# A float32 transformer pair on one core: how the products of `w_down_2` are split and ordered at the end

## The chip, the cores and the metric

One Trainium2 chip, one of its cores. The time is the device time of one execution in microseconds (us); the kernel before took 1609.27 us in the median of three runs (1608.09 to 1610.73).

## The reference, cut to what matters

Two transformer blocks on one sequence of 512 tokens with a model width of 1024. The change touches only the end of the second block, its MLP:

```python
h2 = rmsnorm(x, mlp_norm_w[l])
u = jax.nn.relu(jnp.einsum('bld,df->blf', h2, w_up[l]))
x = x + jnp.einsum('blf,fd->bld', u * u, w_down[l])
return rmsnorm(x, final_norm_w)
```

Here `w_up_2` is 1024 x 4096 and `w_down_2` is 4096 x 1024, both float32.

## The kernel before

The program writes an instruction stream for each engine by hand, with semaphores between them. Every float32 product is made of three TensorE products in a reduced float format: each operand is split into a high part (`hi`, a rounded copy, made by ScalarE, here called ACT) and a low part (`lo` = operand - `hi`, a subtraction), and `three` (L812 to L814) multiplies hi by hi, hi by lo and lo by hi into the same PSUM bank.

The end of the kernel is a list of 42 steps, `STREAM` (L246), that all engines walk through. There are two kinds of step.

- An **up unit** `("up", q, j)` is 256 columns of `w_up_2`: 48 matmuls for two PSUM banks. VectorE (DVE) takes each bank with a relu into `f` (L2230), and ACT squares it (L1688). Four units make the 1024 hidden columns of set q. The first two units of set 0 lie before the list.
- A **product** `("down", q, n)` is one of the seven products of a Strassen-Winograd scheme that multiplies the 512 x 1024 hidden values of set q by 1024 rows of `w_down_2`: 24 matmuls for two banks. `PRODUCTS` names its operands: token parts A11 to A22 and sums S1 to S4 (128 x 1024 each), weight parts B11 to B22 and sums T1 to T4 (128 x 2048). Products of one chain (`CHAIN`) accumulate in the same two banks, and DVE adds the running sum of a bank to `x` after each product (L2237), so the next product of the chain may start in a bank only once DVE has taken it (`claim_tail`, L1241).

Before a step v can start on PE, its weights need: a load from HBM into one of five 1 MB places (`raw`, `raw_tail`; `load_tail`, issued by SP in the order of the list, each waiting until the low part of the step that held the place is made, and after n = 3 or 4 also until T4 or T3 is made, L717); for a sum, the subtraction on DVE (`weight_sum`, L2249 to L2261); the high part on ACT (`tail_high`, L1664); and the low part. The low part is made on GpSimd (POOL) in two halves of 128 x 1024 (L795, L797), except for n = 2, where DVE makes it in one instruction (`weight_low`, L2297). A product also needs the token part: high on ACT (`token_high`, L1680), low on DVE (`token_low`, L2290), and for S1 to S4 a sum on DVE (`token_sum`, L2271 to L2282).

The order on each engine is written out per step `at_v`: ACT squares the second half of the step before, makes the weights' high part of step `at_v + 2`, then its tokens' high part, then squares the first half of `at_v`. DVE takes the second half of the step before, makes sums, makes the low parts of step `at_v + 2`, and only then takes the first half of `at_v` (loop at L2300). High and low parts have three places each in rotation, so step v + 2 can be prepared once step v has started. The order of the steps is: units of set 0 and 1; the seven products of set 0; four units of set 2; seven products of set 1; four units of set 3; seven products of set 2; seven products of set 3:

```python
for q in range(2, FF2_Q):
    out += down[q - 2] + up[q]
return out + down[FF2_Q - 2] + down[FF2_Q - 1]
```

## Time and profile before

| what | before |
|---|---|
| median of three runs | 1609.27 us |
| the profiled execution, its own time | 1609.46 us |
| its span | 1607.6 us |
| PE busy | 1563.9 us, 97% of the span |
| DVE, ACT, POOL busy | 916.2, 531.6, 790.2 us |
| mean granted TensorE clock | 0.99 |
| the list of 42 steps on PE | 1250 to 1600 us |

The span is what the profiler saw between first and last instruction; the execution's own time is 1.9 us more. In the view of instructions in order of time, the first matmul of set 0 starts at 1315.68 us, the units behind it at 1364.69, set 1 at 1408.21, the units behind it at 1455.87, set 2 at 1499.39, set 3 at 1551.38, and the last matmul's slot ends at 1600.37.

### The profile page before, as it was taken

The numbers are of one execution on the slowest core, as the hardware profiler recorded it, in microseconds if no ns is written. First come the engines' busy times: TensorE is split into PE (matmuls) and PEld (weight loads), VectorE is DVE, ScalarE is ACT, GpSimd is POOL, SyncE is SP. The second block draws the span as 40 slices with busy tenths as digits, with TensorE's granted clock in tenths as the row PEclk, the third lists the DMA queues.
The fourth block names the chain that finished last, engine by engine and source line by source line (L and its number), as shares of the span: only waits on it lengthen the run. The fifth ranks groups of instructions, "written<-read, shape, count | busy, mean of one in ns | idle before, by whom it ended". The sixth has DMA issues, their size and how long they took to land.

```text
span 1607.6 us, 19248 instructions
## 1 busy us (share of the span) xinstructions
PE 1563.9 (97%) x7495; PEld 1286.0 (80%) x7495; DVE 916.2 (57%) x1185; ACT 531.6 (33%) x760; POOL 790.2 (49%) x289
## 2 busy tenths in 40 slices
PE   9999999999999999999999999999999998989886
PEld 7887788888888888888888887877789886868764
DVE  5902588900246666666006489987555156382798
ACT  3012121200135443443124244257433334242334
POOL 5874288677760445445440003421251448556476
PEclk9999999999999999999999999999999999999998
DMA  6232032233242332332232232221232503214021
GB/s 223 90 120 79 1 112 92 92 105 105 79 131 80 105 105 79 104 104 89 95 118 73 89 97 79 81 52 26 80 131 79 183 27 127 83 56 154 0 79 53
DMA packets 127382, 147.00 MB, mean 91 GB/s; under 512 B 5143, under 2 KB 98375, under 8 KB 127304
## 3 DMA queue, kind: packets, MB, share of 16 engines
q1 hardware_dynamic: 125430, 141.05, 27.9%
q10 hardware_dynamic: 1874, 4.85, 0.9%
q8 instruction: 55, 0.90, 0.3%
q14 instruction: 23, 0.19, 0.0%
HBM read 143.79 MB, written 2.10 MB: 91 GB/s over the span
## 4 chain that ended last, share of the span: by engine, by line
PE 85%; POOL 5%; DVE 4%; issue 3%; ACT 2%; DMA 1%; POOLq 0%; DVEq 0%; SPq 0%; ACTq 0%
PE ps L812 26%; PE ps L814 25%; PE ps L813 25%; PE ps L967 3%; PE ps L1042 2%; POOL w_lo L795 1%; POOL w_lo L797 1%; PE ps L1209 1%; POOL w_lo L759 1%; PE ps L1030 1%; POOL tail_lo L795 1%; PE ps L1226 1%; DVE a_lo L2290 1%; POOL w_hi L754 1%; DVE x L2237 1%
## 5 line engine op out<-in xcount | busy, mean ns | idle before, releaser
L759 POOL TENSOR_TENSOR w_lo<-raw,w_hi 128x1024 fp32r<-128x1024 f32 x166 | 420.5, 2554 | 496.4 <-ACT w_hi L1312 493.6
L812 PE MATMUL ps<-hT_hi,w_hi 128*128 128x512 f32 (+1 forms) x848 | 324.5, 383 | 0.8 <-POOL w_lo L759 0.5
L813 PE MATMUL ps<-hT_lo,w_hi 128*128 128x512 f32 (+1 forms) x848 | 323.2, 381 | 0.0
L814 PE MATMUL ps<-hT_hi,w_lo 128*128 128x512 f32 (+1 forms) x848 | 323.2, 381 | 0.0
L754 POOL TENSOR_TENSOR w_hi<-raw,cells 128x2048 fp32r<-128x2048 f32 x35 | 129.5, 3701 | 126.5 <-PE ps L812 125.3
L812 PEld LDWEIGHTS ps<-hT_hi,w_hi 128*128 128x128 f32 x848 | 159.4, 188 | 33.9 <-issue 2.3
L814 PEld LDWEIGHTS ps<-hT_hi,w_lo 128*128 128x128 f32 x848 | 159.4, 188 | 30.6
L813 PEld LDWEIGHTS ps<-hT_lo,w_hi 128*128 128x128 f32 x848 | 159.4, 188 | 30.4
L1312 ACT ACTIVATE w_hi<-raw 128x2048 fp32r<-128x2048 f32 (+1 forms) x58 | 109.6, 1890 | 128.3 <-PE ps L812 106.5
L812 PE MATMUL ps<-w_hi,hT_hi 128*128 128x512 f32 (+2 forms) x400 | 151.6, 379 | 0.0
L813 PE MATMUL ps<-w_lo,hT_hi 128*128 128x512 f32 (+2 forms) x400 | 150.1, 375 | 0.0
L814 PE MATMUL ps<-w_hi,hT_lo 128*128 128x512 f32 (+2 forms) x400 | 150.1, 375 | 0.0
L1787 DVE TENSOR_TENSOR w_lo<-raw,w_hi 128x1024 fp32r<-128x1024 f32 (+1 forms) x20 | 22.0, 1144 | 144.4 <-ACT w_hi L1312 144.4
L812 PEld LDWEIGHTS ps<-w_hi,hT_hi 128*128 128x128 f32 x400 | 75.4, 189 | 13.7 <-POOL w_lo L778 0.5
L814 PEld LDWEIGHTS ps<-w_hi,hT_lo 128*128 128x128 f32 x400 | 75.4, 188 | 13.3
L813 PEld LDWEIGHTS ps<-w_lo,hT_hi 128*128 128x128 f32 x400 | 75.4, 189 | 12.7
L812 PE MATMUL ps<-w_hi,a_hi 128*128 128x512 f32 x152 | 63.9, 421 | 18.8 <-POOL w_lo L797 18.8
L2290 DVE TENSOR_TENSOR a_lo<-f,a_hi 128x1024 fp32r<-128x1024 f32 x24 | 58.3, 2429 | 33.4 <-ACT a_hi L1680 33.4
L795 POOL TENSOR_TENSOR w_lo<-raw,w_hi 128x1024 fp32r<-128x1024 f32 x12 | 32.7, 2721 | 90.1 <-ACT w_hi L1664 90.1
L2230 DVE TENSOR_SCALAR f<-ps 128x512 f32<-128x512 f32 x28 | 19.0, 687 | 86.5 <-PE ps L814 86.5
L795 POOL TENSOR_TENSOR w_lo<-raw_tail,w_hi 128x1024 fp32r<-128x1024 f32 x14 | 44.7, 3194 | 40.0 <-ACT w_hi L1664 39.9
L813 PE MATMUL ps<-w_lo,a_hi 128*128 128x512 f32 x152 | 62.5, 411 | 0.0
(368 smaller groups left out, 3161.7 us busy)
## 6 DMA issues: line engine op xcount, KB each, us to landing
raw<-in_w_in SPq DMA_DIRECT2D x86, 512.0 KB, 4.7
raw<-in_w_up SPq DMA_DIRECT2D x60, 512.0 KB, 4.8
raw<-in_w_down SPq DMA_DIRECT2D x34, 512.0 KB, 4.2
raw_tail<-in_w_down SPq DMA_DIRECT2D x20, 512.0 KB, 4.7
raw<-in_w_out SPq DMA_DIRECT2D x16, 512.0 KB, 4.2
raw_tail<-in_w_up SPq DMA_DIRECT2D x16, 512.0 KB, 4.9
raw<-in_w_ret_o SPq DMA_DIRECT2D x8, 512.0 KB, 4.0
raw<-in_w_sgu_o SPq DMA_DIRECT2D x8, 512.0 KB, 4.0
```

The lines of the kernel that those rows point to most:

```text
L754: nc.gpsimd.tensor_tensor(hi[:, 0:n], raw[:, s, 0:n], zero.broadcast_to([P, n]), ALU.add).then_inc(unit_hi, 1)
L759: nc.gpsimd.tensor_tensor(lo[:, c], raw[:, s, c], hi[:, c].bitcast(f32), ALU.subtract).then_inc(unit_split, 1)
L795: nc.gpsimd.tensor_tensor(lo[:, 0:UNIT // 2], tail_raw_of(v)[:, 0:UNIT // 2], hi[:, 0:UNIT // 2].bitcast(f32), ALU.subtract)
L812: first = nc.tensor.matmul(dst, a_hi, b_hi, start=start, stop=False, skip_group_check=onto)
L813: nc.tensor.matmul(dst, a_hi, b_lo, start=False, stop=False, skip_group_check=onto)
L814: return first, nc.tensor.matmul(dst, a_lo, b_hi, start=False, stop=stop, skip_group_check=onto)
L967: last = nc.tensor.transpose(ps[:, BANK[t], n * width:n * width + width], src, ident[0:k, 0:k])
L1042: last = nc.tensor.matmul(ps[:, BANK[t], nn * 256:nn * 256 + 256], sT[:, h % 2, mb, n0:n0 + P], v[:, mb, h * RET_DV:(h + 1) * RET_DV], sta ...
L1312: nc.scalar.activation(slot_of(u)[0][:, 0:n], raw[:, s, 0:n], ACT.Copy).then_inc(hi_given, 1)
L1787: V.tensor_tensor(lo[:, c], raw[:, u % 2, c], hi[:, c].bitcast(f32), ALU.subtract).then_inc(unit_split, 1)
L2230: V.tensor_scalar(f2[q % 2][:, c, :], ps[:, TAIL_BANK[e], :], 0.0, None, ALU.max).then_inc(tail_taken, 1)
L2290: V.tensor_tensor(a_lo[:, a_n % A_SLOTS, :, :], tokens_of(q, PRODUCTS[n].split()[0]), a_hi[:, a_n % A_SLOTS, :, :].bitcast(f32), ALU.subtr ...
```

## The change

Four of the seven low parts of a set (n = 2, 3, 5, 6) are made on DVE in place of one; POOL keeps n = 0, 1 and 4, and all up units. The seven products of sets 1 and 2 no longer stand together: the units of the set after next stand between them (`BETWEEN`). Sets 0 and 3 are still seven products in a row. On ACT the tokens' high part now comes before the weights' high part of the same step. The sums T2 to T4 are tied to the step before their product; for products in a row that is the same place as before.

```diff
--- before.py
+++ after.py
@@ -230,27 +230,29 @@
 CHAIN = {0: "a", 1: "b", 2: "c", 3: "a", 4: "c", 5: "a", 6: "a"}
 OPENS = (0, 1, 2)
 TO_X = ((0, 0), (0, 0), (2, 1), (0, 1), (0, 1), (2, 1), (2, 0))
-VECTOR_LOW = 2
+VECTOR_LOW = (2, 3, 5, 6)
+BETWEEN = (("up", 0), ("down", 0), ("down", 1), ("up", 1), ("down", 2), ("down", 3), ("up", 2), ("down", 4), ("up", 3),
+           ("down", 5), ("down", 6))
 
 
 def second_mlp():
 
     up = [[("up", q, j) for j in range(4)] for q in range(FF2_Q)]
     down = [[("down", q, n) for n in range(7)] for q in range(FF2_Q)]
-    out = up[0][2:] + up[1]
-    for q in range(2, FF2_Q):
-        out += down[q - 2] + up[q]
-    return out + down[FF2_Q - 2] + down[FF2_Q - 1]
+    out = up[0][2:] + up[1] + down[0]
+    for q in range(1, FF2_Q - 1):
+        out += [up[q + 1][n] if kind == "up" else down[q][n] for kind, n in BETWEEN]
+    return out + down[FF2_Q - 1]
 
 
 STREAM = second_mlp()
-START = [STREAM.index(("down", q, 0)) for q in range(FF2_Q)]
+AT = {step: v for v, step in enumerate(STREAM)}
 RAW_SLOTS, W_SLOTS, A_SLOTS = 5, 3, 3
 
 
 def low_count(v):
 
-    by_vector = [kind == "down" and n == VECTOR_LOW for kind, _, n in STREAM]
+    by_vector = [kind == "down" and n in VECTOR_LOW for kind, _, n in STREAM]
     return by_vector[v], by_vector[:v + 1].count(by_vector[v])
 
 
@@ -1673,7 +1675,7 @@
                 else:
                     act.wait_ge(tokens_added, 4 * q + TOKEN_SUMS.index(name) + 1)
                 if a_n >= A_SLOTS:
-                    before = START[(a_n - A_SLOTS) // 7] + (a_n - A_SLOTS) % 7
+                    before = AT["down", (a_n - A_SLOTS) // 7, (a_n - A_SLOTS) % 7]
                     act.wait_ge(tail_started, before + 2)
                 else:
                     act.wait_ge(tail_started, 1)
@@ -1697,9 +1699,9 @@
                 if at_v:
                     square(at_v - 1, 1)
                 if at_v + 2 < N:
-                    tail_high(at_v + 2)
                     if STREAM[at_v + 2][0] == "down":
                         token_high(at_v + 2)
+                    tail_high(at_v + 2)
                 square(at_v, 0)
             root_table()
             for tt in range(2):
@@ -2245,18 +2247,18 @@
                 if name == "T1":
                     await_loaded(dve, "down", q, "B11")
                     await_loaded(dve, "down", q, "B12")
-                    await_low(dve, START[q])
+                    await_low(dve, AT["down", q, 0])
                     made = V.tensor_tensor(out, raw_part(q, "B12"), out, ALU.subtract)
                 elif name == "T2":
                     await_loaded(dve, "down", q, "B22")
-                    await_low(dve, START[q] + 2)
+                    await_low(dve, AT["down", q, 2])
                     made = V.tensor_tensor(out, raw_part(q, "B22"), out, ALU.subtract)
                 elif name == "T3":
                     await_loaded(dve, "down", q, "B22")
                     dve.wait_ge(weights_added, 4 * q + 1)
                     made = V.tensor_tensor(out, raw_part(q, "B22"), out, ALU.subtract)
                 else:
-                    await_low(dve, START[q] + 1)
+                    await_low(dve, AT["down", q, 1])
                     dve.wait_ge(weights_added, 4 * q + 2)
                     made = V.tensor_tensor(out, out, raw_part(q, "T2"), ALU.subtract)
                 made.then_inc(weights_added, 1)
@@ -2301,21 +2303,20 @@
                 if at_v:
                     take(at_v - 1, 1)
                 kind, q, n = STREAM[at_v]
-                coming = next((c for c in range(FF2_Q) if START[c] - at_v in (1, 2)), None)
-                if kind == "down" and n == 0:
-                    token_sum(q, "S2")
-                elif kind == "down" and n == 1:
-                    token_sum(q, "S4")
-                if kind == "down" and 1 <= n <= 3:
-                    weight_sum(q, ADDS[n])
+                coming = next((c for c in range(FF2_Q) if AT["down", c, 0] - at_v in (1, 2)), None)
+                if kind == "down" and n < 2:
+                    token_sum(q, TOKEN_SUMS[2 + n])
                 if coming is not None:
-                    token_sum(coming, TOKEN_SUMS[2 - (START[coming] - at_v)])
+                    token_sum(coming, TOKEN_SUMS[2 - (AT["down", coming, 0] - at_v)])
+                nearest = STREAM[at_v + 1]
+                if nearest[0] == "down" and 2 <= nearest[2] <= 4:
+                    weight_sum(nearest[1], ADDS[nearest[2] - 1])
                 if at_v + 2 < N and STREAM[at_v + 2][0] == "down":
                     token_low(at_v + 2)
-                if coming is not None and START[coming] - at_v == 1:
+                    if low_count(at_v + 2)[0]:
+                        weight_low(at_v + 2)
+                if coming is not None and AT["down", coming, 0] - at_v == 1:
                     weight_sum(coming, "T1")
-                if kind == "down" and n == 0:
-                    weight_low(at_v + 2)
                 take(at_v, 0)
 
             def root(tt):
```

The new order of steps from the first product on is: set 0, n = 0 to 6; up (2,0); set 1 n = 0, 1; up (2,1); n = 2, 3; up (2,2); n = 4; up (2,3); n = 5, 6; up (3,0); set 2 n = 0, 1; up (3,1); n = 2, 3; up (3,2); n = 4; up (3,3); n = 5, 6; set 3, n = 0 to 6. The loads follow the list. Before, the load of up (2,3) waits only for the low part of set 0's n = 5, with five steps in between; now it waits for the low part of set 1's n = 3 and for T4 of set 1, made at the step two ahead of it. The same holds for up (3,3) and set 2.

**DVE, set 0, from T2 to the low parts of n = 6.** Before (`raw` of L2253 is T2, `raw_tail` of L2257 and L2261 are T3 and T4):

```order
L2253 TENSOR_TENSOR raw<-raw_tail_136,raw 128x2048
L2290 TENSOR_TENSOR a_lo<-f_0_131,a_hi 128x1024
L2237 TENSOR_TENSOR x<-ps,x 128x512 x2
L2257 TENSOR_TENSOR raw_tail_135<-raw_tail_136,raw_tail_135 128x2048
L2290 TENSOR_TENSOR a_lo<-f_0_131,a_hi 128x1024
L2237 TENSOR_TENSOR x<-ps,x 128x512 x2
L2261 TENSOR_TENSOR raw_tail_134<-raw_tail_134,raw 128x2048
L2290 TENSOR_TENSOR a_lo<-s_141,a_hi 128x1024
L2237 TENSOR_TENSOR x<-ps,x 128x512 x2
L2290 TENSOR_TENSOR a_lo<-f_0_131,a_hi 128x1024
```

Now (lines are two or more further down: L2255, L2259, L2263 are T2 to T4, L2299 is `weight_low`):

```order
L2255 TENSOR_TENSOR raw<-raw_tail_136,raw 128x2048
L2292 TENSOR_TENSOR a_lo<-f_0_131,a_hi 128x1024
L2299 TENSOR_TENSOR w_lo<-raw,w_hi 128x2048
L2239 TENSOR_TENSOR x<-ps,x 128x512 x2
L2259 TENSOR_TENSOR raw_tail_135<-raw_tail_136,raw_tail_135 128x2048
L2292 TENSOR_TENSOR a_lo<-f_0_131,a_hi 128x1024
L2239 TENSOR_TENSOR x<-ps,x 128x512 x2
L2263 TENSOR_TENSOR raw_tail_134<-raw_tail_134,raw 128x2048
L2292 TENSOR_TENSOR a_lo<-s_141,a_hi 128x1024
L2299 TENSOR_TENSOR w_lo<-raw_tail_135,w_hi 128x2048
L2239 TENSOR_TENSOR x<-ps,x 128x512 x2
L2292 TENSOR_TENSOR a_lo<-f_0_131,a_hi 128x1024
L2299 TENSOR_TENSOR w_lo<-raw_tail_134,w_hi 128x2048
```

Three weights' low parts, for n = 3, 5 and 6, have come in, each between the tokens' low part and the adds of a bank to `x` (L2237, now L2239).

**DVE, set 1, around T4.** Before, with the products in a row (L2261 is T4, the adds on both sides are of n = 2 to 5, `f` of L2230 is up (3,0)):

```order
L2261 TENSOR_TENSOR raw<-raw,raw_tail_134 128x2048
L2290 TENSOR_TENSOR a_lo<-s_141,a_hi 128x1024
L2237 TENSOR_TENSOR x<-ps,x 128x512 x2
L2290 TENSOR_TENSOR a_lo<-f_1_132,a_hi 128x1024
L2237 TENSOR_TENSOR x<-ps,x 128x512 x6
L2230 TENSOR_SCALAR f_1_132<-ps 128x512 x4
L2271 TENSOR_TENSOR s_141<-f_0_131 128x1024
```

Now, from the adds ahead of the tokens' low part of n = 4 to the weights' low part of n = 6 (L2263 is T4, L2232 takes up (2,2) and (2,3)):

```order
L2239 TENSOR_TENSOR x<-ps,x 128x512 x2
L2292 TENSOR_TENSOR a_lo<-f_1_132,a_hi 128x1024
L2239 TENSOR_TENSOR x<-ps,x 128x512 x2
L2263 TENSOR_TENSOR raw_tail_136<-raw_tail_136,raw 128x2048
L2232 TENSOR_SCALAR f_0_131<-ps 128x512 x2
L2292 TENSOR_TENSOR a_lo<-s_141,a_hi 128x1024
L2299 TENSOR_TENSOR tail_lo_138<-raw_tail_135,tail_hi_137 128x2048
L2239 TENSOR_TENSOR x<-ps,x 128x512 x2
L2292 TENSOR_TENSOR a_lo<-f_1_132,a_hi 128x1024
L2299 TENSOR_TENSOR w_lo<-raw_tail_136,w_hi 128x2048
```

T4 is now behind the add of n = 3, at up (2,2). The adds of n = 4 (the row of L2239 after the low part of n = 5) stand behind both low parts of n = 5, and up (2,3) uses the banks of n = 4.

## Rows read from the trace of the kernel before

**Rows 1.** The page, part 1: busy time of each engine, share of the span, instructions.
```profile
PE 1563.9 (97%) x7495; PEld 1286.0 (80%) x7495; DVE 916.2 (57%) x1185; ACT 531.6 (33%) x760; POOL 790.2 (49%) x289
```

**Rows 2.** Busy time by stretch, cut where the sets of products begin and end.
```profile
core 0: us, PE busy (x) PEld busy (x) DVE busy (x) ACT busy (x) POOL busy (x), PEclk, DMA share, GB/s
1315.68:1364.69 49.01, 42.04 (x169) 33.56 (x168) 35.39 (x27) 19.15 (x14) 33.80 (x11) 0.93 0.29 90
1364.69:1408.21 43.52, 43.52 (x193) 36.04 (x192) 16.14 (x12) 13.02 (x12) 23.38 (x10) 1.00 0.28 92
1408.21:1455.87 47.66, 41.83 (x169) 33.45 (x168) 35.40 (x27) 19.15 (x14) 32.45 (x11) 0.93 0.27 89
...
1499.39:1551.38 51.99, 42.48 (x169) 33.52 (x168) 45.66 (x31) 21.03 (x16) 36.78 (x11) 0.93 0.18 61
1551.38:1600.37 48.99, 41.51 (x169) 32.79 (x167) 42.94 (x35) 18.57 (x22) 32.26 (x10) 0.93 0.05 20
```

**Rows 3.** Waits of PE alone, 1225 to 1608 us: total, times, longest.
```profile
PE ps L812 <- POOL w_lo L797: 18.8, 6, 5.6
PE ps L812 <- POOL tail_lo L797: 8.3, 4, 4.4
PE ps L812 <- DVE x L2237: 2.7, 1, 2.7
```

**Rows 4.** Instructions in time, PE, first matmuls after three stalls: start us, us, engine, line.
```profile
1336.61 0.80 PE L812 MATMUL ps<-w_hi,a_hi 128*128 128x512 f32 x1 [4.45 <-POOL w_lo L797]
...
1535.76 0.50 PE L812 MATMUL ps<-w_hi,a_hi 128*128 128x512 f32 x1 [1.98 <-POOL w_lo L797]
...
1573.62 0.80 PE L812 MATMUL ps<-w_hi,a_hi 128*128 128x512 f32 x1 [5.57 <-POOL w_lo L797]
```

**Rows 5.** Busy time and granted clock (PEclk) in three short stretches.
```profile
1336.40:1339.80 3.40, 3.19 (x8) 2.54 (x9) 3.40 (x2) 1.06 (x1) 3.40 (x2) 0.50 0.00 0
...
1533.50:1541.00 7.50, 5.52 (x25) 4.33 (x24) 7.43 (x7) 2.86 (x2) 7.50 (x3) 1.00 0.97 349
...
1572.00:1578.70 6.70, 5.08 (x12) 4.03 (x13) 6.70 (x3) 2.86 (x2) 6.70 (x3) 0.50 0.00 0
```

**Rows 6.** Instructions in time, DVE, the first set.
```profile
1311.64 4.48 DVE L2249 TENSOR_TENSOR raw<-raw_tail,raw 128x2048 f32<-128x2048 f32 x1
...
1320.78 1.22 DVE L2290 TENSOR_TENSOR a_lo<-f,a_hi 128x1024 fp32r<-128x1024 f32 x1 [2.32 <-ACT a_hi L1680]
1321.92 2.28 DVE L2297 TENSOR_TENSOR w_lo<-raw,w_hi 128x2048 fp32r<-128x2048 f32 x1
1324.12 1.41 DVE L2237 TENSOR_TENSOR x<-ps,x 128x512 f32<-128x512 f32 x2
...
1335.59 3.11 DVE L2257 TENSOR_TENSOR raw_tail<-raw_tail,raw_tail 128x2048 f32<-128x2048 f32 x1
1338.62 3.42 DVE L2290 TENSOR_TENSOR a_lo<-f,a_hi 128x1024 fp32r<-128x1024 f32 x1
```

**Rows 7.** Instructions in time, POOL, the first set.
```profile
1330.89 2.38 POOL L795 TENSOR_TENSOR w_lo<-raw,w_hi 128x1024 fp32r<-128x1024 f32 x1 [16.91 <-ACT w_hi L1664]
1333.23 3.33 POOL L797 TENSOR_TENSOR w_lo<-raw,w_hi 128x1024 fp32r<-128x1024 f32 x1
...
1344.26 4.46 POOL L795 TENSOR_TENSOR w_lo<-raw_tail,w_hi 128x1024 fp32r<-128x1024 f32 x1
```

**Rows 8.** Instructions in time, ACT, the first set.
```profile
1316.76 1.23 ACT L1688 ACTIVATE f<-f 128x512 f32<-128x512 f32 x2 [7.66 <-DVE f L2230]
1317.90 1.90 ACT L1664 ACTIVATE w_hi<-raw 128x2048 fp32r<-128x2048 f32 x1
1319.70 1.04 ACT L1680 ACTIVATE a_hi<-f 128x1024 fp32r<-128x1024 f32 x1
```

**Rows 9.** Loads of raw (a 1 MB unit alone), then raw_tail (two units together): landing.
```profile
DMA to landing us min/median/max: 3.9/4.4/4.9
...
DMA to landing us min/median/max: 4.9/6.2/7.2
```

## The prediction

> **What bounds the kernel now.** I read the page's busy times first. TensorE (PE) is busy 97% of the span [rows 1], so only what PE waits for can be won. The change acts from the first product on, so I cut the trace there [rows 2]. Four units between two sets take 43.52 us with PE never idle: 10.88 us a unit of 48 matmuls, 0.227 us each, at the full clock. A product has 24, so 5.44 us, and a set of seven 38.1 us. The sets take 49.0, 47.7, 52.0 and 49.0 us. So they lose 10.9, 9.6, 13.9 and 10.9 us, 45.3 in all, the most that any order can win. Two thirds of it is idle time: PE waits 27.1 us for low parts from POOL and 2.7 for an add to `x` on DVE [rows 3]. The rest, some 14 us, is clock: the granted mean is 0.93 in each set of some 49 us [rows 2], that is half speed for about 7 us, which costs 3.4 a set.
>
> **Why the low parts are late.** POOL needs 2.38 us for a half, and 3.33 or 4.46 when DVE works beside it [rows 7]. On DVE the same happens: tokens' low parts take 1.22 or 3.42 us, sums of 2048 take 2.28 (as the low part in L2297 does) or 3.11, and T1 4.48 [rows 6]. The excess is the rest of the other engine's instruction: T3 asks at 1335.59, POOL's half ends at 1336.56, T3 ends 2.2 us later, and POOL's next half then runs its full time. So the two take turns at SBUF, one whole instruction each, and adds from PSUM (0.69 each, 1.41 for two) take no turn. A POOL low part is 2 x 2.38 = 4.76 us alone, 7.8 (3.33 + 4.46) between DVE's instructions; PE needs one per 5.44.
>
> **Part one: three more low parts a set on DVE.** Twelve move, each 4.76 us of turns to 2.28. I follow set 0 through the code order with these durations (successive instructions on an engine overlap by 0.08, ACT needs 1.90 for weights, 1.04 for tokens, 0.63 for a square [rows 8]; a bank can be taken 0.4 after its last matmul's slot). Times are those of the trace, so set 0 starts at 1315.68.
> - n = 3: ACT now makes tokens first, so DVE's tokens' low part of n = 1 runs before POOL's turns and T1 takes 2.3, not 4.48. T2 ends at 1327.1 instead of 1328.9, its high part at 1329.0, its low part on DVE at 1331.3. PE wants it at 1332.0: the 4.45 us stall [rows 4] is gone.
> - n = 4: POOL's two halves, T3 and the tokens' low part take turns, 1331.8 to 1339.9. PE wanted it at 1337.4: 2.5 us late.
> - n = 5: adds, T4, two low parts and then the add of n = 3, whose bank it uses, end at 1347.4: 2.05 late.
> - n = 6: the same bank wait, 0.45 late. The set ends at 1358.8 after 43.1 us instead of 49.0: **-5.9**.
>
> Two stalls of over 2 us may halve the clock. At n = 4 that is covered by DVE's chain, at n = 5 not wholly: **+1.0**.
>
> **Part two: units between products.** From up (2,0) to the end of set 1 PE has 43.5 + 38.1 = 81.6 us of work, before 43.5 + 47.7 = 91.2 with stalls. POOL's turns (7 x 4.76 = 33) and DVE's (31.6: seven tokens' low parts, eight instructions of 2048, four token sums) fit into 81.6 easily. But the chain at two steps doesn't:
> - up (2,1): T1, behind four turns at up (2,0), ends at 1372.3; the takes of up (2,0) follow, the square at 1374.9, which stands on ACT ahead of this unit's high part (1376.8), then POOL with S4 and a tokens' low part between: 1383.2. PE wants it at 1380.6: 2.6 late.
> - up (2,3): its load waits for T4, which I place at 1410.4. The later half of a load lands 4.9 us after its issue when the unit is alone, 7.2 with another behind it [rows 9], and here others are; I take 6 between. The high part is done at 1418.3. Behind it on ACT are two squares and the tokens and weights of n = 5, to 1422.2; POOL and DVE take turns; DVE's low part of n = 5 ends at 1426.4 and only then comes the add of n = 4, whose bank up (2,3) uses: 1427. PE wants to start at 1421.3: 5.5 late (5.0 to 6). Such a stall halves the clock for 3.4 us [rows 5], 1.7 more.
>
> With half of a 1.7 for the clock after the shorter stall, and a little for a second dip, I count +1.0. Set 1's stretch: 81.6 + 2.6 + 5.5 + 1.7 + 1.0 = 92.4, so **+1.2**. Set 2's has the same pattern; up (3,1) is 1.4 to 2.6 late, I take 2.0: 81.6 + 2.0 + 5.5 + 1.7 + 0.9 = 91.7, before 43.5 + 52.0 = 95.5: **-3.8**.
>
> **Part three: set 3.** Its n = 0 and 1 are prepared under set 2's last two products, 10.9 us, not under a unit of 10.88 each. POOL's four halves take turns with S1, T1 and two tokens' low parts, so n = 1 starts 2.1 us late, T1 ends 5.2 us into the set, and T2 and its low part at 20.9 us where PE wants 18.4: 2.5 late. Then, as in set 0, 3.1, 2.05 and 0.5 late. It ends after 48.4 us, +1.0 for the clock, before 49.0: **+0.4**.
>
> **Other edits.** The waits on `AT` in place of `START` name the same steps for sets in a row and cost nothing. SP's other loads have 3 to 5 steps, each 5.44 or 10.88 us, against at most 7.2 us from issue to landing [rows 9], so PE covers them; if that cover went, ACT would stand at the load, as it does at up (2,3). POOL's own idle time, where the low parts are gone, is worth nothing by itself. The end behind the last matmul is as before.
>
> **Sum.** -5.9 + 1.0 + 1.2 - 3.8 + 0.4 = -7.1 us. The profiled execution took 1609.46, the median 1609.27, 0.2 lower. So 1602.2, said as **1602.0**. No row shows the new order, so each stall has bounds. From below: the two bank stalls and the unit stalls fall away, which is the second case. From above: every half of POOL pays 4.46 and every load 7.2, the fourth case.
>
> A rule on the clock would cost more. The rows show 3.4 us at 1.2 GHz after 4.45 us of waiting, 6.7 after 5.57, and no fall after 1.98 [rows 4, 5]. The Trainium skill, "TensorE: Matmul & The Clock Gate", section "A second HAM failure mode: psum-queue depth-cycling", says that cycling through PSUM banks with short idle times between groups of matmuls makes the clock swing between half and full. By it each of my ten stalls would bring a dip and the sum would be about 2 us higher, 1604; the trace agrees for the long stalls and not for the 1.98.
>
> **Rivals.**
> 1. *Forecast, 0.50:* the chains above, 1597 to 1605.9.
> 2. *The stalls between units don't come, 0.24.* For it: POOL and DVE have some 17 us free of turns in each stretch of 81.6, and PE is never idle between sets now [rows 2]. Against it: the chain over T4, load, ACT and bank is in the code whatever the averages say. It takes away 2.6 + 5.5 + 2.7 and 2.0 + 5.5 + 2.6 us, 20.9 in all: 1581; with only the two long ones gone (14.4), 1588. Next to this stands a rule: all that is moved counts, 12 x (4.76 - 2.28) = 29.8 us, which gives 1579.7. The Trainium skill, "GPSIMD Engine Reference", section 4.1, sends elementwise work to VectorE, since GpSimd is about twice as slow with two inputs; the trace agrees on the price (4.76 against 2.28), not on its all lying on PE's path. I fold it into this case.
> 3. *Nothing is left, 0.12.* n = 4 to 6 of sets 0 and 3 are DVE's chain as soon as POOL isn't late: T4, tokens, weights, takes. If each of these six is 1 us later than I have it, -7.1 becomes about -1: 1608, within 0.2% of before (1606.05 to 1612.5), about what a measurement can tell.
> 4. *The fourth unit is late by more than the sets win, 0.14.* Place: up (2,3) and up (3,3). Price: landing after 7.2 instead of 6 (+1.2), POOL's halves at 3.33 and 4.46 with the low part of n = 5 behind each (+2.9), and 6.7 us of half clock as in [rows 5] instead of 3.4 (+1.7): 5.8 twice, and the same turns with a full dip at up (2,1) and (3,1), 2.0 each: 15.6 us over the forecast, 1617.6. It decides from where both units start over 10 us late. That the load can't start before T4 speaks for it, that POOL is otherwise idle there against it.
>
> That the change doesn't do what it says I exclude: the order of DVE's instructions has the new low parts and PE's list follows from the same table.
>
> **How the numbers follow.** Faster by over 0.2% (below 1606.05): cases 1 and 2, 0.74. Within: 0.12. Slower: 0.14. The range leaves out the lower tail of case 2 and the upper of case 4: 1584 to 1611; the forecast's own range is 1597 to 1606.
>
> **What would show it.** Right: set 0 takes 43 to 44 us with no wait at n = 3 and waits of some 2.5 and 2 us at n = 4 and 5, the latter put down to DVE. A wait of 5 to 6 us at the fourth unit of sets 2 and 3, ended by DVE's add to `x`, with ACT idle on a DMA into raw ahead of it. Set 3 at 48 to 50 us, T1 there slower than 2.3. DVE's busy time rises by 5 to 25 us (12 x 2.28, less shorter turns), POOL's falls by 55 to 80 (12 x 4.76 and up). Wrong: no wait at the fourth units (case 2), a clock of 1.00 in the stretches of sets 1 and 2, or a wait of over 10 us there (case 4).

## Result and profile after

The changed kernel takes 1593.86 us (median of four runs, 1593.42 to 1594.65), the kernel before 1608.68 us beside it (1607.78 to 1610.73): 14.8 us less, a ratio of 0.9907 with a 95% interval of 0.9889 to 0.9924. The forecast was 7.1 us less, 1602.0 us. The sign held, and the time lies inside the wide range of 1584 to 1611, but not in the forecast's own of 1597 to 1606: it fell between the first case and the second. The gain is twice as large as forecast.

Part 1 of the page of the changed kernel, busy time of each engine:

```profile
PE 1559.0 (98%) x7495; PEld 1283.3 (81%) x7495; DVE 935.2 (59%) x1197; ACT 532.2 (33%) x760; POOL 713.9 (45%) x265
```

Against [rows 1], DVE's busy time is 19 us longer (12 x 2.28 = 27, less shorter turns) and POOL's 76 us shorter, both within what was forecast. PE is busy 98% of a span that is 14.7 us shorter.

The same stretches as [rows 2], cut where they begin and end now: set 0; the units (2,j) and set 1, interleaved; the units (3,j) and set 2; set 3.

```profile
core 0: us, PE busy (x) PEld busy (x) DVE busy (x) ACT busy (x) POOL busy (x), PEclk, DMA share, GB/s
1314.95:1358.19 43.24, 40.26 (x170) 32.53 (x169) 40.84 (x29) 20.81 (x15) 15.56 (x5) 0.96 0.32 111
1358.19:1448.31 90.12, 85.34 (x361) 69.45 (x360) 61.89 (x42) 31.94 (x26) 39.37 (x15) 0.96 0.28 92
1448.31:1537.67 89.36, 84.04 (x362) 68.56 (x361) 65.09 (x44) 32.05 (x26) 38.73 (x15) 0.98 0.24 78
1537.67:1585.79 48.12, 41.12 (x169) 32.12 (x167) 46.89 (x39) 19.13 (x22) 13.94 (x4) 0.96 0.06 22
```

One set is 38.1 us of matmuls, a set with four units 81.6. So the four stretches lose 5.2, 8.5, 7.8 and 10.0 us, 31.5 in all. Before it was 10.9, 9.6, 13.9 and 10.9, 45.3 in all. This is 13.8 us of the 14.7; 0.7 came ahead of set 0, in code that the change doesn't touch. The clock column lets some of it be read off directly: 0.93 in each set before, now 0.96 in set 0 and set 3.

What PE waited for from 1300 us on (in total, times, longest), to set beside [rows 3]:

```profile
PE ps L814 <- DVE x L2239: 14.7, 7, 4.2
PE ps L814 <- DVE w_lo L2299: 2.1, 1, 2.1
PE ps L814 <- POOL w_lo L799: 2.1, 2, 1.6
PE ps L814 <- DVE f L2232: 1.2, 2, 0.6
```

POOL was behind 27.1 of 29.8 us of waiting before and is behind 2.1 of 20.1 now. The adds to `x` on DVE (L2239), 2.7 us in one wait before, have 14.7 in seven. So the waits have changed their owner, and a third of them has gone.

**Set 0.** DVE in order of time, from T1 (L2251) over T2 (L2255), the low parts for n = 3 (tokens L2292, weights L2299), T3 (L2259), the tokens of n = 4 and the adds:

```profile
1307.75 2.28 DVE L2251 TENSOR_TENSOR raw<-raw_tail,raw 128x2048 f32<-128x2048 f32 x1
...
1323.96 2.29 DVE L2255 TENSOR_TENSOR raw<-raw_tail,raw 128x2048 f32<-128x2048 f32 x1
...
1328.23 2.29 DVE L2299 TENSOR_TENSOR w_lo<-raw,w_hi 128x2048 fp32r<-128x2048 f32 x1 [0.85 <-ACT w_hi L1666]
...
1331.77 3.81 DVE L2259 TENSOR_TENSOR raw_tail<-raw_tail,raw_tail 128x2048 f32<-128x2048 f32 x1
1335.50 3.40 DVE L2292 TENSOR_TENSOR a_lo<-f,a_hi 128x1024 fp32r<-128x1024 f32 x1
1338.83 1.40 DVE L2239 TENSOR_TENSOR x<-ps,x 128x512 f32<-128x512 f32 x2
```

T1 takes 2.28 us where it took 4.48 [rows 6], since the tokens' low part of n = 1 came before POOL's turns and not in them. T2 ends at 1326.2, its low part at 1330.5, n = 3 starts on time at 1331.27. T3 (3.81) and the tokens of n = 4 (3.40) each stand one POOL half in line. PE's first matmuls of n = 4 and n = 6:

```profile
1339.65 0.47 PE L814 MATMUL ps<-tail_hi,a_hi 128*128 128x512 f32 x1 [2.78 <-DVE x L2239]
...
1352.62 0.47 PE L814 MATMUL ps<-w_hi,a_hi 128*128 128x512 f32 x1 [0.20 <-DVE x L2239]
```

The n = 4 wait of 2.78 us names the add to `x`, not the low part: its bank is that of n = 2, and that add stands right behind the low part in DVE's line. The set takes 43.24 us; the reckoning without clock reserve gave 43.1.

**The fourth unit of set 2**, where the forecast put its largest loss. Product n = 4 of set 1 starts at 1413.79. ACT, POOL, DVE and PE after it, each in order of time:

```profile
1412.97 1.92 ACT L1666 ACTIVATE w_hi<-raw 128x2048 fp32r<-128x2048 f32 x1 [13.09 <-DMA raw<-in_w_up]
1414.79 1.14 ACT L1690 ACTIVATE f<-f 128x512 f32<-128x512 f32 x2
1415.83 1.04 ACT L1682 ACTIVATE a_hi<-s 128x1024 fp32r<-128x1024 f32 x1
1416.78 1.90 ACT L1666 ACTIVATE tail_hi<-raw_tail 128x2048 fp32r<-128x2048 f32 x1
```

```profile
1414.96 2.41 POOL L797 TENSOR_TENSOR w_lo<-raw,w_hi 128x1024 fp32r<-128x1024 f32 x1 [9.57 <-ACT w_hi L1666]
1417.33 3.36 POOL L799 TENSOR_TENSOR w_lo<-raw,w_hi 128x1024 fp32r<-128x1024 f32 x1
```

```profile
1416.91 1.55 DVE L2292 TENSOR_TENSOR a_lo<-s,a_hi 128x1024 fp32r<-128x1024 f32 x1 [2.22 <-ACT a_hi L1682]
1418.71 4.12 DVE L2299 TENSOR_TENSOR tail_lo<-raw_tail,tail_hi 128x2048 fp32r<-128x2048 f32 x1 [0.26 <-ACT tail_hi L1666]
1422.76 1.40 DVE L2239 TENSOR_TENSOR x<-ps,x 128x512 f32<-128x512 f32 x2
```

```profile
1423.59 0.77 PE L814 MATMUL ps<-hT_hi,w_hi 128*128 128x512 f32 x1 [4.19 <-DVE x L2239]
```

ACT waited 13.09 us for the unit's load. Behind its high part come two squares and the tokens and weights of n = 5. POOL's halves then take turns with DVE, so the weights' low part of n = 5 takes 4.12 us and not 2.28, and the add that frees the bank (L2239) starts only at 1422.76. PE loses 4.36 us from the end of its last matmul's slot, and the granted clock stands at 0.51 from 1422.8 to 1429.6 us: 6.8 us, of which the first 0.8 fall into the wait and the rest costs 3.0. The same stands at up (3,3): 4.24 us of waiting and 1.7 of clock.

### The profile page after: what moved, and what is told of

The parts are those of the page before. It is cut to its first block, busy times and chain, and to the rows that moved or that the text cites. A ratio compares the mean times of both kernels' runs of the same rounds, so it can differ in the third digit from the quotient of the medians.

```text
span 1592.9 us, 19236 instructions
## 1 busy us (share of the span) xinstructions
PE 1559.0 (98%) x7495; PEld 1283.3 (81%) x7495; DVE 935.2 (59%) x1197; ACT 532.2 (33%) x760; POOL 713.9 (45%) x265
## 4 chain that ended last, share of the span: by engine, by line
PE 89%; DVE 5%; issue 3%; ACT 1%; POOL 1%; DVEq 0%; POOLq 0%; ACTq 0%
PE ps L814 27%; PE ps L816 27%; PE ps L815 27%; PE ps L969 3%; PE ps L1044 2%; PE ps L1211 1%; DVE x L2239 1%; DVE a_lo L2292 1%; PE ps L1032 1%; DVE w_lo L2299 1%; PE ps L1228 1%; POOL w_hi L756 1%; PE ps L1103 1%; ACT w_hi L1666 0%; PE ps L1065 0%
## 5 line engine op out<-in xcount | busy, mean ns | idle before, releaser
L761 POOL TENSOR_TENSOR w_lo<-raw,w_hi 128x1024 fp32r<-128x1024 f32 x166 | 420.5, 2554 | 495.9 <-ACT w_hi L1314 493.2
L816 PEld LDWEIGHTS ps<-w_hi,hT_lo 128*128 128x128 f32 x400 | 75.3, 188 | 13.2
L797 POOL TENSOR_TENSOR w_lo<-raw,w_hi 128x1024 fp32r<-128x1024 f32 x10 | 25.8, 2582 | 122.7 <-ACT w_hi L1666 122.6
L814 PE MATMUL ps<-w_hi,a_hi 128*128 128x512 f32 x152 | 60.4, 398 | 6.6 <-DVE x L2239 2.3
L2232 DVE TENSOR_SCALAR f<-ps 128x512 f32<-128x512 f32 x28 | 18.9, 688 | 76.2 <-PE ps L816 76.2
L816 PE MATMUL ps<-w_hi,f_lo 128*128 128x512 f32 x160 | 62.3, 390 | 0.0
L814 PE MATMUL ps<-w_hi,f_hi 128*128 128x512 f32 x160 | 62.3, 390 | 0.0
L815 PE MATMUL ps<-w_lo,f_hi 128*128 128x512 f32 x160 | 62.3, 389 | 0.0
```

The costliest lines, as they stand in the source:

```text
L761: nc.gpsimd.tensor_tensor(lo[:, c], raw[:, s, c], hi[:, c].bitcast(f32), ALU.subtract).then_inc(unit_split, 1)
L797: nc.gpsimd.tensor_tensor(lo[:, 0:UNIT // 2], tail_raw_of(v)[:, 0:UNIT // 2], hi[:, 0:UNIT // 2].bitcast(f32), ALU.subtract)
L814: first = nc.tensor.matmul(dst, a_hi, b_hi, start=start, stop=False, skip_group_check=onto)
L815: nc.tensor.matmul(dst, a_hi, b_lo, start=False, stop=False, skip_group_check=onto)
L816: return first, nc.tensor.matmul(dst, a_lo, b_hi, start=False, stop=stop, skip_group_check=onto)
L2232: V.tensor_scalar(f2[q % 2][:, c, :], ps[:, TAIL_BANK[e], :], 0.0, None, ALU.max).then_inc(tail_taken, 1)
```

## Experiments

Each run's time is given as the difference to the kernel before beside it (1607.8 to 1607.9 us in all of these). The 14.8 us of the changed kernel are against 1608.68; against 1607.85 they would be 14.0, so a difference between a run and the changed kernel that is taken from these numbers is uncertain by 0.8 us. Three letters name the parts of the change: **L**, four low parts a set on VectorE; **B**, units between products; **T**, tokens first on ScalarE. The changed kernel is LBT. Losses by stretch come from one profiled execution each, as above: the length of the stretch less 0.227 us for each of its matmuls. Executions of one kernel differ by up to 4 us, those of LB and B by 6, so a loss is good to one or two us and the losses of LB and B to less.

### The changed kernel with the old order of steps: LT

```diff
-    out = up[0][2:] + up[1] + down[0]
-    for q in range(1, FF2_Q - 1):
-        out += [up[q + 1][n] if kind == "up" else down[q][n] for kind, n in BETWEEN]
-    return out + down[FF2_Q - 1]
+    out = up[0][2:] + up[1]
+    for q in range(2, FF2_Q):
+        out += down[q - 2] + up[q]
+    return out + down[FF2_Q - 2] + down[FF2_Q - 1]
```

> The changed kernel, but with the old order of steps: the seven products of a set in a row everywhere; four low parts a set on VectorE and tokens first on ScalarE are kept. Theory (the gain comes from the low parts on VectorE, and the units between products cost something, through the two waits of over 4 us at up (2,3) and (3,3)): sets 0, 1 and 2 take some 43.2 us each as set 0 does now, units 43.5, set 3 48.1, so about 264.7 us from the first product to the last, against 270.8 in the changed kernel: 1588 us (1586 to 1591). Rival (the units between products carry the gain of sets 1 and 2): these sets lose what they lost before, 9.6 and 13.9 us, instead of 8.5 and 7.8, so 1595 to 1601 us.

Measured: 1591.64 us, -16.2. Between the two. Sets 0 and 1 lose 5.2 us each as the theory had it and set 3 4.5, but set 2, which set 3 follows without a unit, loses 13.2. PE's wait there is 5.4 us at n = 6, for an add to `x`; in DVE's line the sum S1 (2.09 us) and the tokens' low part (3.35 us, with a turn of GpSimd's) of set 3 stand ahead of that add. So with L and T in place the units between products bring nothing: without them the kernel is 1.4 us faster by these differences, at the edge of what can be told.

### Low parts back on GpSimd: BT

```diff
-VECTOR_LOW = (2, 3, 5, 6)
+VECTOR_LOW = (2,)
```

> The changed kernel, but GpSimd makes six low parts a set again, VectorE only that of n = 2; the units stand between the products as changed. Theory: sets 0 and 3 go back to 49 us each with the wait of 4.4 us at n = 3, and sets 1 and 2 with their units hardly move (90 us each), since between units GpSimd's 4.8 us fit: about 1600.5 us (1598 to 1603). Rival (between units too it is the low parts on VectorE that help): sets 1 and 2 go back as well, 1605 us or more.

Measured: 1586.81 us, -21.1, ratio 0.9866 (0.9849 to 0.9882). Both expectations are wrong, and by the sign: they had this run slower than the changed kernel, and it is 6 us faster. The low parts on VectorE, the part of the change named first, cost 6 us here. The stretches of this run (columns as above):

```profile
1315.59:1361.17 45.58, 40.62 (x169) 32.47 (x168) 37.98 (x26) 20.60 (x15) 32.25 (x11) 0.96 0.27 93
1361.17:1443.86 82.69, 81.87 (x362) 67.49 (x361) 53.67 (x39) 32.12 (x26) 61.01 (x21) 1.00 0.32 107
1443.86:1527.08 83.22, 82.19 (x361) 67.42 (x360) 58.40 (x41) 32.13 (x26) 57.30 (x21) 1.00 0.25 84
1527.08:1577.60 50.52, 41.03 (x169) 32.27 (x167) 44.07 (x35) 18.88 (x21) 33.01 (x10) 0.93 0.04 18
```

The units between products with POOL's low parts lose 1.1 and 1.6 us (82.69 and 83.22 less 81.6), at a clock of 1.00, with POOL busy 61 of 83 us. Sets 0 and 3 lose 7.5 and 12.4, 2.3 and 2.4 more than in the changed kernel. So L helps where products stand in a row and harms where units stand between. My theory had expected sets 1 and 2 to stay as they were.

### Weights first on ScalarE: LB

```diff
-                    if STREAM[at_v + 2][0] == "down":
-                        token_high(at_v + 2)
                     tail_high(at_v + 2)
+                    if STREAM[at_v + 2][0] == "down":
+                        token_high(at_v + 2)
```

> The changed kernel, but on ScalarE the weights' high part comes before the tokens' high part, as before the change. Theory (the order on ScalarE is part of the gain, since VectorE makes tokens' low part first and then the weights'): T1 of set 0 meets GpSimd's turns and takes 4.5 us instead of 2.3, and at n = 3 VectorE's low parts wait for the tokens behind the weights, so n = 3 of sets 0 and 3 is 3 us late and later steps in the row take over part of it: 1597 to 1600 us. Rival (the order on ScalarE is hidden): within 1 us of 1593.9.

Measured: 1607.85 us, 0.0, ratio 0.9997 (0.9987 to 1.0007), far beyond the 1597 to 1600 expected. The ten executions scatter: nine lie between 1605.41 and 1611.52 us, one took 2009.55, for which nothing here gives a cause. Without the two swapped lines, which the forecast used but did not price by themselves, the rest of the change brings nothing that can be told by the median. (The profiled execution, 1605.7 us, is 2.2 us below that median, and its losses are too.) ACT and then DVE in set 0 of this run, from T2 on (ACT L1666 weights, L1682 tokens; the first DVE row is T1):

```profile
1328.42 1.92 ACT L1666 ACTIVATE w_hi<-raw 128x2048 fp32r<-128x2048 f32 x1 [8.15 <-DVE raw L2255]
1330.24 1.04 ACT L1682 ACTIVATE a_hi<-f 128x1024 fp32r<-128x1024 f32 x1
```

```profile
1311.16 4.48 DVE L2251 TENSOR_TENSOR raw<-raw_tail,raw 128x2048 f32<-128x2048 f32 x1
...
1326.10 2.28 DVE L2255 TENSOR_TENSOR raw<-raw_tail,raw 128x2048 f32<-128x2048 f32 x1
1331.31 1.23 DVE L2292 TENSOR_TENSOR a_lo<-f,a_hi 128x1024 fp32r<-128x1024 f32 x1 [2.93 <-ACT a_hi L1682]
1332.45 2.29 DVE L2299 TENSOR_TENSOR w_lo<-raw,w_hi 128x2048 fp32r<-128x2048 f32 x1
```

T1 takes 4.48 us again. Then ACT makes T2's high part, then the tokens', and DVE, whose line has tokens ahead of weights, stands until 1331.31 and has the weights' low part done at 1334.7, 4.2 us later than with tokens first. Sets 0 to 2 lose more, 8.5, 9.7 and 14.6 us with their units, set 3 about the same, 9.6.

### The bank freed first: LBT with one add moved

```diff
                     token_low(at_v + 2)
+                    if early:
+                        take(at_v, 0)
                     if low_count(at_v + 2)[0]:
                         weight_low(at_v + 2)
...
-                take(at_v, 0)
+                if not early:
+                    take(at_v, 0)
```

(`early` is true at n = 4 where a unit follows.)

> The changed kernel, with one thing moved on VectorE: at n = 4 of sets 1 and 2 the add of the first half to x, which frees the bank of the unit behind it, comes before the weights' low part of n = 5 and not after. Theory (the bank is what up (2,3) and (3,3) wait for last, the late load stands 2.7 us behind it): their waits fall from 4.2 to about 1.5 us each and their clock dips (3.0 and 1.7 us) fall away: 1584 to 1587 us. Rival (the load, through ScalarE and GpSimd, is the limit, and the bank only comes at the same time): 1592 to 1594 us.

Measured: 1585.29 us, -22.6. As expected by the theory, at the same place:

```profile
1418.03 1.54 DVE L2292 TENSOR_TENSOR a_lo<-s,a_hi 128x1024 fp32r<-128x1024 f32 x1 [2.33 <-ACT a_hi L1682]
1419.49 0.68 DVE L2239 TENSOR_TENSOR x<-ps,x 128x512 f32<-128x512 f32 x1
1420.09 3.85 DVE L2299 TENSOR_TENSOR tail_lo<-raw_tail,tail_hi 128x2048 fp32r<-128x2048 f32 x1
```

```profile
1421.85 0.50 PE L814 MATMUL ps<-hT_hi,w_hi 128*128 128x512 f32 x1 [1.44 <-POOL w_lo L799]
```

The add of one bank (0.68 us) stands ahead of the low part, which takes 3.85; the wait of 4.19 us is 1.44 and is now for POOL's low part of the unit itself. The wait at up (3,3) is 1.21 us. There is no dip of the clock in either stretch's fourth unit. Moving one instruction of 0.7 us is worth 7.8 us (22.6 - 14.8). In the profiled executions the two stretches with units are 5.6 and 4.6 us shorter, and 1.0 us is lost ahead of set 0, in code that the edit doesn't touch.

### Low parts chosen by set

```diff
-    by_vector = [kind == "down" and n in VECTOR_LOW for kind, _, n in STREAM]
+    by_vector = [kind == "down" and n in (VECTOR_LOW if q in (0, FF2_Q - 1) else (2,)) for kind, q, n in STREAM]
```

> The changed kernel, but only sets 0 and 3, whose products stand in a row, have four low parts on VectorE; sets 1 and 2 have one, that of n = 2. New theory (low parts on VectorE help only where products stand in a row and harm where units stand between, since they come ahead of the add that frees a bank): losses of 5.2 us in set 0 (as in the changed kernel), 1.1 and 1.6 in the two stretches of sets 1 and 2 (as in the run with low parts on GpSimd), 10.0 in set 3: 18 us, against 45.3 before: 1582 us. Rival (sets 1 and 2 only look free because set 0 leaves GpSimd its work in another rhythm): losses of 3 us or more in them, 1586 us or more.

Measured: 1581.89 us, -25.9, ratio 0.9837 (0.9821 to 0.9853). The stretches:

```profile
1315.34:1358.56 43.22, 40.03 (x170) 32.28 (x169) 40.84 (x29) 20.82 (x15) 15.75 (x5) 0.96 0.32 111
1358.56:1441.35 82.79, 82.20 (x362) 67.41 (x360) 55.14 (x39) 31.97 (x26) 57.91 (x21) 1.00 0.30 100
1441.35:1524.52 83.17, 82.21 (x362) 67.41 (x361) 58.31 (x41) 32.08 (x26) 57.30 (x21) 1.00 0.25 84
1524.52:1572.63 48.11, 40.82 (x169) 32.17 (x167) 46.88 (x39) 19.11 (x22) 13.93 (x4) 0.96 0.06 22
```

Losses 5.1, 1.2, 1.6 and 10.0: 17.9 where 18 were expected. This version beats both kernels, by 25.9 us and by 11 to 12.

### Tokens first alone: T

The changed kernel with the old order of steps, as in the first run, and

```diff
-VECTOR_LOW = (2, 3, 5, 6)
+VECTOR_LOW = (2,)
```

which leaves tokens first on ScalarE as the one difference to the kernel before.

> The kernel before, with the order on ScalarE alone changed (tokens' high part before the weights'): products in a row, six low parts a set on GpSimd. If the parts of the change simply add up, this alone is worth what taking it out of the changed kernel cost, 14 us: 1594 to 1595 us. If its worth hangs on the rest, I expect what set 0 shows in the run with low parts on GpSimd, a loss of 7.5 us in place of 10.9, and a like step in the others: 1597 to 1600 us.

Measured: 1600.7 us, -7.1, ratio 0.9953 (0.9937 to 0.997). The parts don't add up: this one brings 7 us alone and 15 beside the other two. Sets lose 7.5, 7.5, 9.8 and 12.0 us.

### Units between products alone: B

```diff
-VECTOR_LOW = (2, 3, 5, 6)
+VECTOR_LOW = (2,)
...
-                    if STREAM[at_v + 2][0] == "down":
-                        token_high(at_v + 2)
                     tail_high(at_v + 2)
+                    if STREAM[at_v + 2][0] == "down":
+                        token_high(at_v + 2)
```

> The changed kernel without its low parts on VectorE and without the new order on ScalarE: only the units between products. New theory: sets 1 and 2 lose under 3 us each, since GpSimd's low parts have 81.6 us for 33 us of work and no low part stands ahead of a bank; sets 0 and 3 lose 10.9 and 12 to 13: about 1590 us (1588 to 1594). Rival (the order on ScalarE is what makes the units between products work): sets 1 and 2 lose 8 us or more each, 1600 us or more.

Measured: 1601.48 us, -6.3 (five executions, 1600.28 to 1606.39). The rival was right: without tokens first, sets 1 and 2 with their units lose 9.3 and 11.0 us, with it 1.1 and 1.6. The profiled execution was the slowest of the five, 4.9 us above their median, so these losses are too high for a usual one; how the 4.9 are spread isn't known. At n = 4 of set 1, which starts at 1424.16, ACT and DVE of this run (L1666 weights of n = 5, L1682 its tokens; L2292 tokens' low part, L2239 the adds that free the bank):

```profile
1426.66 1.90 ACT L1666 ACTIVATE tail_hi<-raw_tail 128x2048 fp32r<-128x2048 f32 x1
1428.46 1.04 ACT L1682 ACTIVATE a_hi<-s 128x1024 fp32r<-128x1024 f32 x1
```

```profile
1429.54 2.09 DVE L2292 TENSOR_TENSOR a_lo<-s,a_hi 128x1024 fp32r<-128x1024 f32 x1 [4.48 <-ACT a_hi L1682]
1431.54 1.40 DVE L2239 TENSOR_TENSOR x<-ps,x 128x512 f32<-128x512 f32 x2
```

The tokens' high part comes behind the late load's and the weights', DVE stands still for 4.48 us for it with the add of n = 4 behind it, and up (2,3) waits 2.61 us for that bank.

### Low parts on VectorE alone: L

The changed kernel with the old order of steps, as in the first run, and weights first:

```diff
-                    if STREAM[at_v + 2][0] == "down":
-                        token_high(at_v + 2)
                     tail_high(at_v + 2)
+                    if STREAM[at_v + 2][0] == "down":
+                        token_high(at_v + 2)
```

> The kernel before with the three more low parts a set on VectorE alone: products in a row, weights first on ScalarE. New theory (behind the weights' high part the tokens' come late, and VectorE's low parts wait in line behind that): sets in a row lose 8.5 us as set 0 does in the run with weights first, set 2 some 16: a total near 41 in place of 45.3, 1604 to 1607 us. My reckoning of the prediction, in which 5.9 us of set 0 came from the low parts and T1's order together, would give 1600 us or less.

Measured: 1605.53 us, -2.3, in the range of the new theory. Sets lose 8.5, 8.5, 16.5 and 8.6.

### B with the add moved

The kernel of B, and:

```diff
+                early = kind == "down" and n == 4 and STREAM[at_v + 1][0] == "up"
+                if early:
+                    take(at_v, 0)
                 if at_v + 2 < N and STREAM[at_v + 2][0] == "down":
                     token_low(at_v + 2)
...
-                take(at_v, 0)
+                if not early:
+                    take(at_v, 0)
```

> Only the units between products (weights first on ScalarE, low parts on GpSimd), and at n = 4 of sets 1 and 2 VectorE adds the first half to x before it makes the tokens' low part of n = 5. Theory (with weights first the tokens' high part comes behind the late load and the weights, VectorE's tokens' low part waits for it, and the add that frees the bank waits behind that): the waits of 2.6 and 2.4 us and the clock dips of 1.7 and 1.65 us at up (2,3) and (3,3) shrink to under 1.5 us each in all, so 5 to 7 us below the run with only the units between, 1601.5: 1595 to 1597 us. Rival (GpSimd's low part of the unit, behind the late load, is as late): 1600 us or more.

Measured: 1597.1 us, -10.7, so 4.4 us below B by the medians, a little less than expected. The two profiled executions lie 9.3 us apart, since B's was the slowest of its five; set 0, which the edit doesn't touch, differs by 1.2 us between them, and the wait of some 1.8 us behind up (2,1) is followed by a dip in B's and by none here. So only the waits at the fourth units are compared. DVE at n = 4, which starts at 1419.77:

```profile
1422.76 0.69 DVE L2239 TENSOR_TENSOR x<-ps,x 128x512 f32<-128x512 f32 x1 [2.10 <-PE ps L816]
1425.37 2.09 DVE L2292 TENSOR_TENSOR a_lo<-s,a_hi 128x1024 fp32r<-128x1024 f32 x1 [1.91 <-ACT a_hi L1682]
```

The add (0.69) comes 2.6 us ahead of the tokens' low part. PE's wait is 1.05 us and for POOL, where it was 2.61 for DVE. This is one of the waits that tokens first takes away: the bank, through DVE's order. It is 4.4 of the 14.8 us by which T improves B; the rest, in set 0 and behind up (2,1) and (3,1) among others, was not taken apart.

### T4 and the load early

```diff
+                apart = kind == "down" and n == 3 and nearest[0] == "up"
+                if apart:
+                    weight_sum(q, "T4")
-                if nearest[0] == "down" and 2 <= nearest[2] <= 4:
+                if nearest[0] == "down" and 2 <= nearest[2] <= (3 if kind == "up" else 4):
```

> The changed kernel, with T4 of sets 1 and 2 made at n = 3 and not at the unit behind it, so that the load of the fourth unit can start some 5 us earlier; VectorE's order of low part and add at n = 4 stays. Theory (the load adds to the wait, though the bank is what ends it, because GpSimd's halves then take turns with VectorE's low part of n = 5, 4.12 us instead of 2.28): the waits of 4.2 us shrink to 2.0 to 2.5 and part of the clock dips goes: 1587 to 1590 us. Rival (the load has no part in it): 1593 to 1594 us.

Measured: 1586.94 us, -20.9. ACT and DVE at the same place as in the changed kernel:

```profile
1407.54 1.92 ACT L1666 ACTIVATE w_hi<-raw 128x2048 fp32r<-128x2048 f32 x1 [7.45 <-DMA raw<-in_w_up]
...
1415.46 1.04 ACT L1682 ACTIVATE a_hi<-s 128x1024 fp32r<-128x1024 f32 x1
```

```profile
1416.54 1.23 DVE L2292 TENSOR_TENSOR a_lo<-s,a_hi 128x1024 fp32r<-128x1024 f32 x1 [1.65 <-ACT a_hi L1682]
1418.35 2.29 DVE L2299 TENSOR_TENSOR tail_lo<-raw_tail,tail_hi 128x2048 fp32r<-128x2048 f32 x1 [0.58 <-ACT tail_hi L1666]
1420.56 1.41 DVE L2239 TENSOR_TENSOR x<-ps,x 128x512 f32<-128x512 f32 x2
```

The unit's high part is at 1407.54, not 1412.97; POOL's two halves no longer meet DVE's low part, so the low part of n = 5 takes 2.29 us and not 4.12, and the add comes 2.2 us sooner. The waits are 1.79 and 1.78 us where they were 4.2, and in this execution no dip follows. So the late load and the order of DVE's line make the loss together: taking away either saves 6 to 8 us, the waits being under 2 us and the two dips gone in both profiled executions.

### Two more divisions of the low parts

By set, and in set 3 that of n = 1 on VectorE too:

```diff
-    by_vector = [kind == "down" and n in VECTOR_LOW for kind, _, n in STREAM]
+    by_vector = [kind == "down" and n in ((2, 3, 5, 6), (2,), (2,), (1, 2, 3, 5, 6))[q] for kind, q, n in STREAM]
```

> The version with low parts chosen by set, and in set 3 that of n = 1 on VectorE too. In set 3 of that version n = 1 starts 1.75 us late, behind four halves on GpSimd that take turns with S1, T1 and two tokens' low parts. Theory (turn-taking with GpSimd): with VectorE making it in 2.2 us the start of n = 1 is on time and T1 meets no turn, so set 3 loses 7 to 8 us instead of 10: 1579 to 1580 us. Rival (VectorE's line itself is what is late in set 3): T1 comes 2.2 us later and the gain at n = 1 is lost at n = 2 and 3: 1581.5 to 1583 us.

Measured: 1581.6 us, -26.2, no change that can be told from 1581.89, as the rival had it: n = 1 is on time, the 1.6 us wait there has gone, but n = 3 waits 3.19 us where it waited 2.18, and the set loses 9.2 us in place of 10.0. VectorE's line is what is late there.

By set, with n = 2 and 3 alone in sets 0 and 3:

```diff
-    by_vector = [kind == "down" and n in VECTOR_LOW for kind, _, n in STREAM]
+    by_vector = [kind == "down" and n in ((2, 3), (2,), (2,), (2, 3))[q] for kind, q, n in STREAM]
```

> The version with low parts chosen by set, but in sets 0 and 3 only n = 2 and 3 on VectorE, n = 5 and 6 back on GpSimd. Theory (what counts in a row is the way from T2 to n = 3; n = 4 to 6 cost about the same on either engine, 4.8 us in turns or 2.2 in VectorE's line ahead of the add): set 0 loses 4.5 to 6 us where it lost 5.1, set 3 9 to 11: 1581 to 1583.5 us. Rival (each low part on VectorE in a row saves its 2.5 us of turns): 4 low parts back cost 10 us, 1590 us or more.

Measured: 1583.19 us, -24.6, in the range of the theory. Set 0 loses 5.4 us in place of 5.1, set 3 11.9 in place of 10.0, more than the 9 to 11 expected. So in set 0 n = 3 is nearly all the worth of L (with no low part moved it lost 7.5). In set 3 it is not: there it brings 0.5 us of 2.4 (12.4 with none moved), and n = 5 and 6 the rest. The theory holds for one of the two rows.

## Why the forecast had the sign and the longest waits right, and the size and its source wrong

All eight combinations of the three parts have been run, each against the kernel before beside it:

| parts | us less than before | losses of the four stretches, us |
|---|---|---|
| none | 0 | 10.9, 9.6, 13.9, 10.9 |
| L | 2.3 | 8.5, 8.5, 16.5, 8.6 |
| T | 7.1 | 7.5, 7.5, 9.8, 12.0 |
| B | 6.3 | 10.9, 9.3, 11.0, 10.8 |
| L, T | 16.2 | 5.2, 5.2, 13.2, 4.5 |
| L, B | 0.0 | 8.5, 9.7, 14.6, 9.6 |
| B, T | 21.1 | 7.5, 1.1, 1.6, 12.4 |
| L, B, T (the change) | 14.8 | 5.2, 8.5, 7.8, 10.0 |

The losses of B are those of an execution 4.9 us slower than its median; those of LB of one 2.2 us faster.

The step that failed is part two, the units between products. Its terms 2.6 and 2.0 us at up (2,1) and (3,1) measured 0.2 and 0.6, its 5.5 at each fourth unit measured 4.4, and with reserves for the clock these two stretches were forecast 4.6 us too dear. The second failure is in the account of the gain: it was put down to low parts moved to DVE and to the units between, and the swap on ACT had no term of its own. The runs show that without the swap nothing is left, and that beside the other two parts the moved low parts cost 6 us.

Point by point, by the steps of the prediction:

- **Part one, set 0: -5.9 + 1.0, measured -5.8.** The chain held to 0.1 us at n = 3 (low part at 1330.5 in the trace; forecast 1331.3, 0.7 of it the earlier start) and the wait there is gone. The +1.0 for the clock was not needed: the one dip, at n = 4, took the place of the wait at n = 5, as the forecast had for n = 4. What failed is the name. I put the gain under "three more low parts on DVE"; the runs give 3.4 of the 5.7 us to tokens first alone (T: 7.5) and 2.4 to L alone (8.5). That T1 is shorter by the order on ACT was in the working, that this was the larger part was not.
- **Part two, set 1's stretch: +1.2, measured -1.1; set 2's: -3.8, measured -6.1.** This is where most of the missing gain lies, 4.6 of 7.7 us. The step up (2,1) and (3,1) was sized 2.6 and 2.0 us late; they start 0.2 and 0.6 late. In my line of turns T1 ended 13.5 us after up (2,0) started, in the trace 12.4 (1370.57 against 1358.19); the high part behind it ended 1.9 us sooner than in my line and POOL's last half 2.5. The step after it, n = 2 behind up (2,1), lost 0.9, most of it waiting for DVE to take that unit's bank (L2232); I had it on time. At the fourth units I had 5.5 us, measured 4.4: T4 ended 0.8 us sooner against the time at which PE wants the unit, and the load was used 5.35 us after its issue (1407.62 to 1412.97), not 6. The clock cost 3.0 and 1.7 us, against 2.7 and 2.6 with my reserves.
- **Part three, set 3: +0.4, measured -0.9.** n = 1 is 1.8 us late and n = 3 2.3, against 2.1 and 2.5; n = 4 3.6 with its clock dip in it, then 1.4 and 0.7. The set lost 10.0 where I had 10.3 and 1.0 for the clock.
- **Sum: -7.1, measured -14.8.** The stretches give -4.9, +1.2, -3.8, +0.4 against -5.8, -1.1, -6.1, -0.9. Every term came out 0.9 to 2.3 us too dear. 0.7 us lies ahead of set 0 and in no term. I had added clock reserves of 3.9 us beyond the two dips at the fourth units, of which 1.3 came on top, in the longer dip at up (2,3); and where two instructions asked for a turn I gave it to the other engine each time. I also let DVE take a bank 0.4 us after its last slot, where the traces have 0.2 to 0.3. Errors to one side add up over ten waits.
- **Rivals.** The second, that the stalls between units don't come, held at up (2,1) and (3,1) and not at the fourth units; BT shows that there too it holds once L is left out, with 1.1 and 1.6 us lost in the stretches. Its "against", that the chain is in the code, needed DVE's weights' low part in front of the add, and the late load. The rule of "all that is moved counts", 29.8 us from 12 low parts, is refuted: with B and T in place those 12 moves cost 6.3 us. The fourth case didn't come: 4.4 us at the fourth unit, not over 10. The sentence on clock swings in the Trainium skill, "TensorE: Matmul & The Clock Gate", section "A second HAM failure mode: psum-queue depth-cycling", would have made ten dips as the prediction read it; the trace has four, behind waits of 2.78, 4.19, 4.24 and 2.14 us, and none behind 1.71 or 1.59.

**What each part does.** Shown by runs: between units L puts a low part of up to 4.1 us ahead of an add that frees a bank (the run with one add moved); in set 0 it shortens the way from T2 to n = 3; B beside T brings the losses of sets 1 and 2 from 7.5 and 9.8 us to 1.1 and 1.6, and without T far less (9.3 and 11.0 in B, 9.7 and 14.6 in LB). Read from traces, and shown by a run for one wait alone: T puts the tokens' high part ahead of what is late, so DVE, which makes tokens first, doesn't stand with the add of a bank behind it. Open: set 2 loses 13.2 us in LT while set 3 loses 4.5. The trace puts 5.4 of it on set 3's S1 and tokens ahead of an add at n = 6, but no run takes it apart. The version by set with the add moved or T4 early wasn't tried.

## What to carry to other kernels

Before you price moving work to a faster engine, look at what stands behind it in that engine's line: an add of 0.7 us that frees a PSUM bank was worth 7.8 us when moved ahead of a low part. Take a change apart into all its edits, the two-line ones too; here nothing of the gain was left without the swap of two high parts, which alone brought 7 us, and one of the two named parts took away 6. When a chain of ten waits is worked out, keep the doubtful turns and reserves on both sides; here, all on one side, they made up most of the 7.7 us that the forecast fell short.
